# Stacked operand for the gate units of a 64-token tile, and another order of gate units and routing tables

## The chip, the cores and the metric

The kernel runs on one core of a Trainium2 chip. The metric is the device time of one execution in microseconds (us), lower is better. A core has TensorE (PE in the rows: matmuls; its loads of the stationary operand are PEld), VectorE (DVE), ScalarE (ACT), GpSimd (POOL) and SyncE (SP), which here only issues transfers, and 16 DMA engines.

## What is computed

One decoder layer for 512 prompt tokens and 64 sample tokens (8 sequences of 8), D = 1024: attention and a gated short convolution, a projection and a layer norm; then for the normalised tokens `x2` a mixture of experts (64 experts, 6 per token), a shared expert and per-layer embeddings, and a second norm. What matters here is the second half, cut:

```
x2 = h.reshape(n * s, D_MODEL)
eidx, gw = route(x2, lw['w_router'], lw['router_bias'])
ffn = (swiglu(x2, lw['w_s_gate'], lw['w_s_up'], lw['w_s_down'])
       + routed_experts(x2, eidx, gw, lw['w_e_gate'], lw['w_e_up'], lw['w_e_down']))
ple = jax.nn.sigmoid(h @ lw['w_ple_gate']) * (p @ lw['w_ple_proj'])
h = layer_norm(DN_ALPHA * h + ffn.reshape(n, s, D_MODEL) + ple, lw['ln2_g'], lw['ln2_b'])
```

The change touches the product `h @ w_ple_gate` and its sigmoid.

## The kernel before

Every engine has its own program, written out by hand in one order; semaphores join them. The 576 tokens are five tiles, four of 128 and one of 64 (`NT` = 5, the last tile has `NS` = 64). Float32 products are made from split operands: each operand is a high part and a low part (`_hi`, `_lo`), and a product is the sum of three terms, high by high, high by low, low by high.

**Gate units.** The product with `w_ple_gate` is cut into 4 blocks of 256 columns (`GW`) and 5 token tiles: 20 units, numbered u = 5 * block + tile. A unit (`gate_unit`, L1399 to L1412) is 8 chunks of the contraction times 3 terms, 24 matmuls, with the tokens as the stationary operand (128 columns, or 64 for the last tile) and 256 columns of weights moving. Its bank of PSUM is one of two (`gate_bank`), so a unit waits until the sigmoid of the unit two before has read it (`u_sig`). Then Scalar takes the sigmoid into `sig_g` (`gate_sigmoid`, L979 to L986), GpSimd multiplies with the projected embeddings (`ple_product`, `u_mul`), and Vector adds the result to the residual (`ppo_add`). The weights of a block are loaded by SyncE (`load_gate`), Scalar makes the high part (`gate_hi`), Vector the low part (`gate_lo`, `pw_lo`). Two slots hold them, so the load of block 3 waits for unit 9, the last of block 1.

**Block 3** (units 15 to 19) is done in two halves: `last_block(True)` makes the two terms with high tokens for all five tiles, three of them in banks of `att`, and ends with `tb_used`; then the gathered tokens of the first expert pass are turned (`turn(0)`); then `last_block(False)` adds the term with low tokens.

**Routing tables.** Vector builds ten tables, each for three of the 30 (tile, choice) pairs (loop at L2013, rows L2021 to L2028), in two buffers; a table waits until TensorE has multiplied the one two before (`tb_used`). TensorE sums them (`table_products`, L1394) between gate units: `N_AHEAD` = 3 units stand before the first table, and one unit follows each of tables 1, 3, 5 and 7 (`UNIT_AFTER`). Before table 4 Vector also makes the second product of the shared expert (`shared_act(1)`). Behind the tables Vector does `gate_lo(2)`, turns the sums into index tables and raises `routed`.

**Transfers.** SyncE issues in one fixed order; a wait holds back everything behind it:

```
sp.wait_ge(routed, 1)
load_parts(1, 1, range(3))
sp.wait_ge(u_ready, 2 * NT)
load_gate(3)
sp.wait_ge(ppo_added, 1)
load_parts(1, 1, range(3, 5))
sp.wait_ge(hs_hd, 1)
load_parts(1, 1, range(5, 6))
sp.wait_ge(tb_used, NTK // TPAIR + 1)
load_parts(2, 2, range(2))
sp.wait_ge(u_ready, N_BLK * NT)
load_parts(2, 2, range(2, 4))
```

Experts are taken in 32 pairs; the weights of a pair are 6 transfers of 1 MB (gate, up, down, for two experts), in a ring of three slots. Each transfer of a pair also waits until the same part of the pair before has landed. From pair 3 on, a load waits until the pair that held its slot has been used.

**A form that is already there.** In the projection with `w_o`, the 64-token tile is stacked: `smp` holds its 64 high and 64 low columns side by side, a matmul multiplies both at once (`packed` in `tile_products`), and Vector adds the lower 64 rows of the result to the upper.

Of the kernel before, what the change touches and what calls it, by code (L numbers as in the profile page):

```python
# [12 lines left out]
ALU = mybir.AluOpType  # L13
# [42 lines left out]
N_AHEAD = 3  # L56
UNIT_AFTER = (1, 3, 5, 7)
# [64 lines left out]
def decoder_step(nc, x_prompt, x_sample, p_prompt, p_sample, win_k, win_v, conv_state, w_in, sinks,  # L122
# [4 lines left out]
    with ctx:  # L127
# [5 lines left out]
        def sem(name):  # L133
            return ctx.enter_context(nc.semaphore(name))
# [131 lines left out]
        pt_lo = at("pt_lo", [P, 2, T], F32R, o_x + 36352)  # L266
        ppo = [at(f"ppo{i}", [P, NT, 512], F32, o) for i, o in enumerate((o_w1 + 28672, o_w2 + 36864))]
# [135 lines left out]
        pw_in = [sem(f"pw_in{i}") for i in range(2)]  # L403
        pw_hi, pw_lo = sem("pw_hi"), sem("pw_lo")
# [88 lines left out]
        def _(sp):  # L493
# [144 lines left out]
            sp.wait_ge(u_ready, N_BLK * NT)  # L638
# [134 lines left out]
        def _(act):  # L773
# [188 lines left out]
            gate_hi(0)  # L962
            act.wait_ge(lt_mm, 1)
# [16 lines left out]
            def gate_sigmoid(u):  # L980

                w = ntok(u % NT)
                act.wait_ge(u_ready, u + 1)
                if u >= NSIG:
                    act.wait_ge(u_mul, u - NSIG + 1)
                nc.scalar.activation(sig_g[0:w, u % NSIG, :], gate_bank(u)[0:w, :], ACT.Sigmoid).then_inc(u_sig, 1)  # L986
# [59 lines left out]
        def _(pe):  # L1046
# [351 lines left out]

            def gate_unit(u):  # L1399

                j, t = u // NT, u % NT
                w = ntok(t)
                if t == 0:
                    pe.wait_ge(pw_lo, j + 1)
                whi, wlo = (m[GATE_SLOT[j]][:, :].rearrange("p (c n) -> p c n", c=KC) for m in (pg_hi, pg_lo))
                if u >= 2:
                    pe.wait_ge(u_sig, u - 1)
                for c in range(KC):
                    for n, (x, v) in enumerate(((xt_hi, whi), (xt_hi, wlo), (xt_lo, whi))):
                        last = nc.tensor.matmul(gate_bank(u)[0:w, :], x[:, c, t * P:t * P + w], v[:, c, :],  # L1410
                                                start=(c == 0 and n == 0), stop=(c == KC - 1 and n == 2))
                last.then_inc(u_ready, 1)  # L1412
# [11 lines left out]
            def last_block(high):  # L1424

                whi, wlo = (m[GATE_SLOT[3]][:, :].rearrange("p (c n) -> p c n", c=KC) for m in (pg_hi, pg_lo))
                terms = ((xt_hi, whi), (xt_hi, wlo)) if high else ((xt_lo, whi),)
                for t in range(NT):
                    u, w = 3 * NT + t, ntok(t)
                    if high and t == 3:  # L1430
                        pe.wait_ge(u_sig, 3 * NT)
                    for c in range(KC):
                        for n, (x, v) in enumerate(terms):
                            last = nc.tensor.matmul(gate_bank(u)[0:w, :], x[:, c, t * P:t * P + w], v[:, c, :],
                                                    start=(high and c == 0 and n == 0), stop=(not high and c == KC - 1))
                    if not high:
                        last.then_inc(u_ready, 1)
                if high:
                    last.then_inc(tb_used, 1)
# [138 lines left out]
        def _(dve):  # L1578
# [434 lines left out]

            for m in range(NTK // TPAIR):
# [3 lines left out]
                if m >= 2:  # L2018
# [10 lines left out]
                                        ALU.mult).then_inc(tb_ready, 1)  # L2029
            gate_lo(2)  # L2030
# [23 lines left out]
            dve.drain().then_inc(routed, 1)  # L2054

# [19 lines left out]
            for u in range(2 * NT, 3 * NT):  # L2075
                ppo_add(u)
            xt_half(0)
            for u in range(3 * NT, N_BLK * NT):
                last = ppo_add(u)
# [142 lines left out]
```

## Time and profile before

| | us |
|---|---|
| median of 3 runs | 1253.28 |
| lowest, highest | 1251.75, 1253.85 |
| the profiled execution | 1250.78 |
| its span, first to last instruction | 1248.9 |
| TensorE busy in it | 1214.2 (97%) |
| Vector busy in it | 505.8 (40%) |
| Scalar busy in it | 318.7 (26%) |
| GpSimd busy in it | 140.4 (11%) |
| moved by DMA | 307.31 MB, mean 246 GB/s |

TensorE is busy over the whole span, since its pipelined matmuls overlap in the records: the busy share doesn't say that it is the bound. Rows give a start in us from the span's start, a duration, the engine, the line and the operation. The start-to-start distance of matmuls is what a stream costs.

### The profile page before, as it was taken

To read this page: it belongs to the slowest core of one execution; us is meant where nothing else is said; L and a number is where in the kernel's file an instruction comes from. 1 tells how busy PE (TensorE), PEld (TensorE's weight loads), DVE (VectorE), ACT (ScalarE), POOL (GpSimd) and SP (SyncE) were. 2 spreads that over 40 slices of the span, in tenths; PEclk is the share of its full clock that TensorE was granted. 3 is DMA by queue.
4 is the path that set the end of the run, shared out by engine and by line. 5 is a ranking of instruction groups with operands and counts; after the bars stand their busy time and mean duration, and the time that the engine had idled before them with its cause. 6 is when DMAs were issued, how large, how long until landed. Compare 5 with 4: busy or idle time off the path is not lost.

```text
span 1248.9 us, 23615 instructions
## 1 busy us (share of the span) xinstructions
PE 1214.2 (97%) x8816; PEld 958.2 (77%) x8817; DVE 505.8 (40%) x1147; ACT 318.7 (26%) x614; POOL 140.4 (11%) x211
## 2 busy tenths in 40 slices
PE   8999999999999999999999999989999999999887
PEld 8999979999999999998999565556555555556543
DVE  4666783432444323567973112211222222121137
ACT  4364653322211222316012111111111111111121
POOL 0200000000000000003024212111121121221200
PEclk9999999999999999999999999999999999999999
DMA  8222223223222232606347999999999999999996
GB/s 266 79 62 68 68 52 68 68 67 102 68 86 84 68 120 67 213 21 211 146 172 297 420 418 420 421 420 419 420 420 419 422 419 418 420 422 420 421 374 290
DMA packets 98656, 307.31 MB, mean 246 GB/s; under 512 B 11244, under 2 KB 62404, under 8 KB 72840
## 3 DMA queue, kind: packets, MB, share of 16 engines
q1 hardware_dynamic: 85332, 275.20, 56.9%
q0 software_dynamic: 12304, 28.60, 5.9%
q10 hardware_dynamic: 948, 2.50, 0.6%
q8 instruction: 52, 0.85, 0.3%
q14 instruction: 20, 0.16, 0.0%
HBM read 294.45 MB, written 26.94 MB: 257 GB/s over the span
## 4 chain that ended last, share of the span: by engine, by line
PE 49%; DMA 42%; DVE 6%; issue 1%; DVEq 1%; ACT 0%; SPq 0%; POOL 0%; ACTq 0%; POOLq 0%
DMA w_exp<-in_w_e_down_dram 40%; PE proj L1060 32%; PE proj L1270 4%; PE proj L1410 3%; PE att L1192 1%; PE att L1154 1%; PE att L1279 1%; PE proj L1094 1%; DMA fold<-expert_rows 1%; PE att L1205 1%; DVE res L2155 1%; PE att L1270 1%; PE proj L1394 1%; DMA expert_rows<-ysb,sidx_col 1%; DMA x_tok<-in_x_prompt_dram 1%
## 5 line engine op out<-in xcount | busy, mean ns | idle before, releaser
L1481 PE MATMUL att<-w_exp,xt 128*64 128x256 f32 x2560 | 286.3, 380 | 8.7 <-DMA w_exp<-in_w_e_up_dram 6.6
L1481 PEld LDWEIGHTS att<-w_exp,xt 128*64 128x64 f32 x2560 | 189.8, 137 | 114.9 <-issue 36.0
L1060 PE MATMUL proj<-h_hi,w_hi 128*128 128x288 f32 x768 | 167.8, 300 | 0.3 <-DVE w_lo L475 0.3
L1060 PE MATMUL proj<-h_hi,w_lo 128*128 128x288 f32 x768 | 164.0, 295 | 0.0
L1060 PE MATMUL proj<-h_lo,w_hi 128*128 128x288 f32 x768 | 163.9, 295 | 0.0
L1501 PE MATMUL proj<-w_exp,ht_e 128*64 128x512 f32 x640 | 146.2, 598 | 3.8 <-DMA w_exp<-in_w_e_down_dram 3.8
L1060 PEld LDWEIGHTS proj<-h_hi,w_hi 128*128 128x128 f32 x768 | 122.3, 189 | 6.1 <-issue 4.6
L1060 PEld LDWEIGHTS proj<-h_lo,w_hi 128*128 128x128 f32 x768 | 123.6, 188 | 0.0
L1060 PEld LDWEIGHTS proj<-h_hi,w_lo 128*128 128x128 f32 x768 | 123.4, 188 | 0.0
L475 DVE TENSOR_TENSOR w_lo<-w_raw,w_hi 128x2048 fp32r<-128x2048 f32 x33 | 75.6, 2291 | 93.1 <-ACT w_hi L465 88.5
L1501 PEld LDWEIGHTS proj<-w_exp,ht_e 128*64 128x64 f32 x640 | 43.6, 136 | 76.4 <-issue 72.1
L465 ACT ACTIVATE w_hi<-w_raw 128x2048 fp32r<-128x2048 f32 x33 | 63.1, 1911 | 84.5 <-PE proj L1060 73.9
L2102 DVE TENSOR_SCALAR ysb<-proj,tabw 128x512 f32 x40 | 30.0, 751 | 131.7 <-PE proj L1501 131.7
L2097 DVE TENSOR_TENSOR h_e<-sg,att 128x128 f32<-128x128 f32 x80 | 19.5, 285 | 116.8 <-PE att L1481 116.8
L2092 DVE TENSOR_TENSOR sg<-sg,att 128x256 f32<-128x256 f32 x40 | 16.9, 421 | 119.9 <-ACT sg L1012 119.9
L1020 ACT ACTIVATE ysb<-proj,tabw 128x512 f32 x40 | 27.5, 688 | 133.3 <-PE proj L1501 133.3
L1015 ACT ACTIVATE ht_e<-att 128x128 f32<-128x128 f32 x80 | 19.0, 278 | 166.6 <-PE att L1487 166.6
L1420 PEld LDWEIGHTS proj<-ident,xg 128*128 128x128 f32 x328 | 43.6, 196 | 16.5 <-issue 13.8
L1060 PE MATMUL proj<-mix_hi,w_lo 128*128 128x288 f32 x256 | 54.8, 296 | 0.0
L1060 PE MATMUL proj<-mix_hi,w_hi 128*128 128x288 f32 x256 | 54.8, 296 | 0.0
L1060 PE MATMUL proj<-mix_lo,w_hi 128*128 128x288 f32 x256 | 54.8, 296 | 0.0
L1420 PE MATMUL proj<-ident,xg 128*128 128x128 f32 x328 | 53.9, 287 | 0.9 <-DMA xg<-x_rows,gidx_col 0.8
(388 smaller groups left out, 1769.1 us busy)
## 6 DMA issues: line engine op xcount, KB each, us to landing
w_exp<-in_w_e_gate_dram SPq DMA_DIRECT2D x64, 1024.0 KB
w_exp<-in_w_e_up_dram SPq DMA_DIRECT2D x64, 1024.0 KB
w_exp<-in_w_e_down_dram SPq DMA_DIRECT2D x64, 1024.0 KB
w_raw<-in_w_in_dram SPq DMA_DIRECT2D x21, 1024.0 KB
part<-expert_rows SPq DMA_DIRECT2D x8, 1536.0 KB, 20.4
w_raw<-in_w_in_dram SPq DMA_DIRECT2D x8, 512.0 KB
w_raw<-in_w_attn_out_dram SPq DMA_DIRECT2D x8, 512.0 KB
w_raw<-in_w_conv_out_dram SPq DMA_DIRECT2D x4, 1024.0 KB
```

Source lines behind the costliest of these rows:

```text
L465: nc.scalar.activation(w_hi[:, g.par, :], w_raw[:, g.par, :], ACT.Copy).then_inc(hi_done, 1)
L475: nc.vector.tensor_tensor(w_lo[:, g.par, :], w_raw[:, g.par, :], w_hi[:, g.par, :].bitcast(F32), ALU.subtract).then_inc(w_ready, 1)
L1015: nc.scalar.activation(ht_e[:, c, :], att[:, 1 - c, 0:P], ACT.Copy).then_inc(ht_ready, 1)
L1020: nc.scalar.activation(ysb[:, bass.ds(side_of, 1), 0:512].rearrange("p o n -> p (o n)"), proj[:, 2, :], ACT.Copy, scale=tabw[:, bass.ds(k, ...
L1060: last = nc.tensor.matmul(proj[:, 2 * i + a, 0:HALF], lhs, x[:, c, a * HALF:(a + 1) * HALF], start=(c == 0 and n == 0), stop=(c == KC - 1 ...
L1270: last = nc.tensor.matmul(out, x, v, start=(c == 0 and n == 0), stop=(c == KC - 1 and n == last_term))
L1410: last = nc.tensor.matmul(gate_bank(u)[0:w, :], x[:, c, t * P:t * P + w], v[:, c, :], start=(c == 0 and n == 0), stop=(c == KC - 1 and n = ...
L1420: last = nc.tensor.transpose(proj[:, half, c * P:(c + 1) * P], xg[:, :, half * 4 + c], ident[:, :])
L1481: last = nc.tensor.matmul(att[e * SLOT:(e + 1) * SLOT, m, 0:FF], xt[:, c, e * SLOT:(e + 1) * SLOT], weights[e][:, c, :], start=(c == 0), s ...
L1501: last = nc.tensor.matmul(proj[e * SLOT:(e + 1) * SLOT, 2 + half, :], ht_e[:, c, e * SLOT:(e + 1) * SLOT], down[e][:, c, half * 512:(half ...
L2097: nc.vector.tensor_tensor(h_e[:, c:FF:2], sg[:, c:FF:2], att[:, 2, c:FF:2], ALU.mult).then_inc(h_ready, 1)
L2102: nc.vector.tensor_scalar(ysb[:, bass.ds(side_of, 1), 512:D].rearrange("p o n -> p (o n)"), proj[:, 3, :], tabw[:, bass.ds(k, 1)], None, A ...
```

## The change

The 64-token tile's units (4, 9, 14 and 19) get a stacked operand. Scalar copies the tile's high and low columns side by side into `xt_both`; a unit (`packed_unit`) is then 16 matmuls of 128 columns, each with both parts: high weights, then low weights. This makes four terms, the low by low one among them. The two halves of the result, rows 0 to 63 and 64 to 127, are added on Vector (`packed_add`: a copy out of PSUM, a drain, an addition) into `sig_g`, and the sigmoid of these units reads `sig_g` instead of PSUM. Vector's program has the four sums at fixed places: after table 3, after `routed`, before the addition of unit 13, and after the turned tokens have been copied. Unit 19 is complete in the high half of block 3, where it comes first.

The order of units and tables is another: four units before the first table, and one unit after each of tables 0, 2, 4 and 6. SyncE's wait for `u_ready` = 20 becomes 19.

```
-N_AHEAD = 3
-UNIT_AFTER = (1, 3, 5, 7)
+N_AHEAD = 4
+UNIT_AFTER = (0, 2, 4, 6)
...
+        xt_both = at("xt_both", [P, KC, 2, NS], F32R, o_x + 36864)
...
+        packed_sum, PACKED_0 = s_sub, 1
...
-            sp.wait_ge(u_ready, N_BLK * NT)
+            sp.wait_ge(u_ready, N_BLK * NT - 1)
...
             gate_hi(0)
+            act.drain()
+            nc.scalar.activation(xt_both[:, :, 0, :], xt_hi[:, :, SEQ:T].bitcast(F32), ACT.Copy)
+            act.wait_ge(x2_lo, 2 * NT)
+            nc.scalar.activation(xt_both[:, :, 1, :], xt_lo[:, :, SEQ:T].bitcast(F32), ACT.Copy)
+            act.drain()
...
+                if u % NT == NT - 1:
+                    act.wait_ge(packed_sum, PACKED_0 + u // NT + 1)
+                    nc.scalar.activation(sig_g[0:w, u % NSIG, :], sig_g[0:w, u % NSIG, :], ACT.Sigmoid).then_inc(u_sig, 1)
+                    return
...
+            def packed_unit(u, whi, wlo):
+
+                for c in range(KC):
+                    both = xt_both[:, c, :, :].rearrange("p a n -> p (a n)")
+                    for n, v in enumerate((whi, wlo)):
+                        last = nc.tensor.matmul(gate_bank(u), both, v[:, c, :],
+                                                start=(c == 0 and n == 0), stop=(c == KC - 1 and n == 1))
+                return last
...
-                for t in range(NT):
-                    u, w = 3 * NT + t, ntok(t)
+                if high:
+                    pe.wait_ge(u_sig, N_BLK * NT - 6)
+                    packed_unit(N_BLK * NT - 1, whi, wlo)
+                for t in range(NT - 1):
+                    u = 3 * NT + t
...
+            def packed_add(u):
+
+                if u == N_BLK * NT - 1:
+                    dve.wait_ge(tb_used, NTK // TPAIR + 1)
+                else:
+                    dve.wait_ge(u_ready, u + 1)
+                dve.wait_ge(u_mul, u - NSIG + 1)
+                o, total = gate_bank(u), sig_g[0:NS, u % NSIG, :]
+                nc.vector.tensor_copy(total, o[NS:P, :])
+                dve.drain()
+                nc.vector.tensor_tensor(total, total, o[0:NS, :], ALU.add).then_inc(packed_sum, 1)
...
+                if m == 3:
+                    packed_add(NT - 1)
...
             dve.drain().then_inc(routed, 1)
+            packed_add(2 * NT - 1)
...
             for u in range(2 * NT, 3 * NT):
+                if u == 3 * NT - 2:
+                    packed_add(3 * NT - 1)
                 ppo_add(u)
             xt_half(0)
+            packed_add(N_BLK * NT - 1)
             for u in range(3 * NT, N_BLK * NT):
```

Vector's program around tables 3 and 4 (`tab_a` and `tab_b` are a table's two operands, `hs_f` the shared expert's product). Before:

```order
L2021 TENSOR_TENSOR tab_b<-cc_152,col_j 128x3x90 [waits tb_used]
L2023 TENSOR_TENSOR tab_a<-cc_152,slot_j 128x384
L2026 TENSOR_TENSOR tab_b<-tab_b,cc_152 128x3x90
L2028 TENSOR_TENSOR tab_b<-tab_b,wj 128x3x90
L1950 TENSOR_TENSOR hs_f<-att,hs_f 128x576 [waits ss_ready]
L1952 TENSOR_TENSOR hs_f<-att,hs_f 128x576
L2021 TENSOR_TENSOR tab_b<-cc_152,col_j 128x3x90 [waits tb_used]
```

Now:

```order
L2058 TENSOR_TENSOR tab_b<-cc_153,col_j 128x3x90 [waits tb_used]
L2060 TENSOR_TENSOR tab_a<-cc_153,slot_j 128x384
L2063 TENSOR_TENSOR tab_b<-tab_b,cc_153 128x3x90
L2065 TENSOR_TENSOR tab_b<-tab_b,wj 128x3x90
L2047 COPY sig_g<-proj 64x256 [waits u_mul,u_ready]
L2049 TENSOR_TENSOR sig_g<-sig_g,proj 64x256
L1975 TENSOR_TENSOR hs_f<-att,hs_f 128x576 [waits ss_ready]
L1977 TENSOR_TENSOR hs_f<-att,hs_f 128x576
L2058 TENSOR_TENSOR tab_b<-cc_153,col_j 128x3x90 [waits tb_used]
```

The sum of unit 4 stands between table 3 and the shared product, with table 4 behind both.

TensorE's program at the last tables (a table is three matmuls, `x2` is a row of two; the row behind them is the first matmul of the next unit). Before, tables 8 and 9 behind unit 6:

```order
L1394 MATMUL proj<-tab_b,tab_a 128x180 [waits tb_ready]
L1394 MATMUL proj<-tab_b,tab_a 128x180 x2
L1394 MATMUL proj<-tab_b,tab_a 128x180 [waits tb_ready]
L1394 MATMUL proj<-tab_b,tab_a 128x180 x2
L1410 MATMUL proj<-pg_hi_150,xt_hi 128x256 [waits u_sig]
```

Now, tables 7, 8 and 9 behind unit 7:

```order
L1405 MATMUL proj<-tab_b,tab_a 128x180 [waits tb_ready]
L1405 MATMUL proj<-tab_b,tab_a 128x180 x2
L1405 MATMUL proj<-tab_b,tab_a 128x180 [waits tb_ready]
L1405 MATMUL proj<-tab_b,tab_a 128x180 x2
L1405 MATMUL proj<-tab_b,tab_a 128x180 [waits tb_ready]
L1405 MATMUL proj<-tab_b,tab_a 128x180 x2
L1432 MATMUL proj<-pg_hi_151,xt_hi 128x256 [waits u_sig]
```

Table 7 has moved behind one more unit, and three tables stand in a row at the end.

## Rows read from the trace of the kernel before

**Rows 1.** Chain of waits (start us, us, what): two TensorE stretches, the first transfer.

```profile
630.27 2.73 PE proj L1410 x24
...
644.25 22.73 PE proj L1410 x192
...
684.67 10.41 DMA w_exp<-in_w_e_down_dram
```

**Rows 2.** Windows: length, busy PE, PEld, DVE, ACT, POOL; clock, DMA share, GB/s.

```profile
652.00:660.00 8.00, 8.00 (x69) 8.00 (x68) 0.54 (x2) 1.15 (x3) 2.34 (x4) 1.00 1.03 400
671.00:677.00 6.00, 6.00 (x54) 6.00 (x53) 0.00 (x0) 0.00 (x0) 0.35 (x1) 1.00 0.45 184
...
820.00:840.00 20.00, 17.60 (x113) 10.14 (x115) 4.22 (x9) 3.22 (x8) 3.86 (x7) 1.00 1.02 421
```

**Rows 3.** Timeline of SyncE's queue: start us, us to issue, line, transfer, count.

```profile
648.05 0.81 SPq L596 DMA_DIRECT2D w_exp<-in_w_e_gate_dram  x2
...
652.76 0.38 SPq L588 DMA_DIRECT2D pg_raw<-in_w_ple_gate_dram  x1
...
676.51 0.81 SPq L596 DMA_DIRECT2D w_exp<-in_w_e_gate_dram  x2
682.14 0.80 SPq L596 DMA_DIRECT2D w_exp<-in_w_e_up_dram  x2
```

**Rows 4.** Timeline of TensorE, 64-token tile stacked in the projection with `w_o`.

```profile
522.65 0.28 PE L1270 MATMUL att<-w_lo,smp 128*128 128x256 f32 x1
...
524.33 0.28 PE L1270 MATMUL att<-w_lo,smp 128*128 128x256 f32 x1
```

**Rows 5.** Timeline of Vector, from table 3 to the low half of gate block 2.

```profile
626.09 0.43 DVE L2021 TENSOR_TENSOR tab_b<-cc,col_j 128x270 f32<-128x270 f32 x1
...
627.94 0.75 DVE L1950 TENSOR_TENSOR hs_f<-att,hs_f 128x576 f32<-128x576 f32 x1
...
629.45 0.51 DVE L2021 TENSOR_TENSOR tab_b<-cc,col_j 128x270 f32<-128x270 f32 x1
...
633.96 0.56 DVE L2021 TENSOR_TENSOR tab_b<-cc,col_j 128x270 f32<-128x270 f32 x1 [0.65 <-PE proj L1394]
...
642.50 2.29 DVE L1893 TENSOR_TENSOR pg_lo<-pg_raw,pg_hi 128x2048 fp32r<-128x2048 f32 x1
```

**Rows 6.** Timeline of TensorE: tables (L1394), gate units (L1410), last block (L1434).

```profile
622.53 1.18 PE L1394 MATMUL proj<-tab_b,tab_a 128*128 128x180 f32 x6 [1.66 <-DVE tab_b L2028]
...
632.84 1.99 PE L1394 MATMUL proj<-tab_b,tab_a 128*128 128x180 f32 x12
634.55 0.41 PE L1410 MATMUL proj<-pg_hi,xt_hi 128*128 128x256 f32 x1
...
637.55 2.00 PE L1394 MATMUL proj<-tab_b,tab_a 128*128 128x180 f32 x12
...
666.81 0.28 PE L1434 MATMUL att<-pg_hi,xt_hi 128*128 128x256 f32 x1
```

**Rows 7.** Timeline of Vector: an addition of 64 tokens by 256 columns.

```profile
653.99 0.42 DVE L2063 SCALAR_TENSOR_TENSOR res<-res,ppo 64x256 f32<-64x256 f32 x1 [1.87 <-POOL ppo L706]
```

**Rows 8.** Timelines of Scalar and Vector: the two splits of gate block 3.

```profile
660.94 1.92 ACT L960 ACTIVATE pg_hi<-pg_raw 128x2048 fp32r<-128x2048 f32 x1 [2.03 <-DMA pg_raw<-in_w_ple_gate_dram]
...
662.88 2.29 DVE L1893 TENSOR_TENSOR pg_lo<-pg_raw,pg_hi 128x2048 fp32r<-128x2048 f32 x1 [8.48 <-ACT pg_hi L960]
```

**Rows 9.** Scalar: the copy into `smp` (by tile), and the logits' copy (timeline).

```profile
L912 ACT ACTIVATE smp<-merged_hi x1: 636/636/636, 508.9 to 508.9; 128x512 fp32r<-128x512 f32 x1
...
584.78 0.65 ACT L964 ACTIVATE lt<-proj 128x576 f32<-128x576 f32 x1 [1.86 <-PE proj L1344]
```

**Rows 10.** Timeline of GpSimd: the first gather of tokens.

```profile
660.80 1.13 POOL L721 DMA_INDIRECT xg<-x_rows,gidx_col  x1 [0.95 <-POOL gidx_col L718]
```

**Rows 11.** Waits of TensorE: us in total, times, longest us.

```profile
PE att L1481 <- DMA w_exp<-in_w_e_up_dram: 6.6, 5, 2.1
...
PE proj L1394 <- DVE tab_b L2028: 2.3, 2, 1.7
```

More of the change, by code:

```diff
@@ L985, in gate_sigmoid @@
                     act.wait_ge(u_mul, u - NSIG + 1)
-                nc.scalar.activation(sig_g[0:w, u % NSIG, :], gate_bank(u)[0:w, :], ACT.Sigmoid).then_inc(u_sig, 1)
+                nc.scalar.activation(sig_g[0:w, u % NSIG, :], gate_bank(u), ACT.Sigmoid).then_inc(u_sig, 1)
             for u in range(N_BLK * NT):
@@ L1397, in table_products @@
                 last.then_inc(tb_used, 1)
+            def packed_unit(u, whi, wlo):
[5 more added lines that the diff above has]
+                return last
             def gate_unit(u):
                 j, t = u // NT, u % NT
-                w = ntok(t)
                 if t == 0:
@@ L1407, in gate_unit @@
                     pe.wait_ge(u_sig, u - 1)
[L1408 to L1411, printed above, removed]
+                if t == NT - 1:
+                    last = packed_unit(u, whi, wlo)
+                else:
+                    for c in range(KC):
+                        for n, (x, v) in enumerate(((xt_hi, whi), (xt_hi, wlo), (xt_lo, whi))):
+                            last = nc.tensor.matmul(gate_bank(u), x[:, c, t * P:(t + 1) * P], v[:, c, :],
+                                                    start=(c == 0 and n == 0), stop=(c == KC - 1 and n == 2))
                 last.then_inc(u_ready, 1)
@@ L1433, in last_block @@
                         for n, (x, v) in enumerate(terms):
-                            last = nc.tensor.matmul(gate_bank(u)[0:w, :], x[:, c, t * P:t * P + w], v[:, c, :],
+                            last = nc.tensor.matmul(gate_bank(u), x[:, c, t * P:(t + 1) * P], v[:, c, :],
                                                     start=(high and c == 0 and n == 0), stop=(not high and c == KC - 1))
@@ L2012, in _ @@
             dve.drain()
+            def packed_add(u):
+                if u == N_BLK * NT - 1:
+                    dve.wait_ge(tb_used, NTK // TPAIR + 1)
+                else:
+                    dve.wait_ge(u_ready, u + 1)
[4 more added lines that the diff above has]
+                nc.vector.tensor_tensor(total, total, o[0:NS, :], ALU.add).then_inc(packed_sum, 1)
             for m in range(NTK // TPAIR):
```

## Prediction

> **What bounds the kernel now.** I read the chain of waits first. From 684.67 us it consists of expert-weight transfers, one behind the other; before that it is TensorE's: the tables and gate units, 22.73 us for the last eight units before the fourth gate block [rows 1]. The windows give the reason: in the expert stage the DMA engines move 421 GB/s at a share of 1.02 while TensorE has room (17.60 of 20 us busy), but from 671 to 677 us they move only 184 GB/s [rows 2]. So the stream of experts cannot be shortened by TensorE, but it can start earlier or later. It starts with the issue of pair 2's gate weights at 676.51 us, which waits for `tb_used` = 11, the end of the high half of the fourth gate block (`last_block(True)`, first matmul at 666.81) [rows 3, 6]. Call that end X. Before the change X is 676.5; what X moves, the end moves, one for one. Work ahead of it counts only if it reaches X.
>
> **What the change removes.** A unit of the 64-token tile had 24 matmuls, 2.73 us [rows 1]; stacked, it has 16 of 128 columns. The kernel already has that form in its third projection: the second stacked matmul starts at 522.65, the last at 524.33, so 14 steps are 1.68 us, 0.12 each [rows 4]. Sixteen make 1.92 us: 0.81 us less. Three of the four such units lie before `last_block(True)`: 2.4 us. The fourth had 16 matmuls in the high half (about 16/24 x 2.73 = 1.82) and now has 16 of 0.12 (1.92): +0.1 us for X; its 8 in the low half (0.9 us) are gone behind X. If nothing else waited, X would come 2.3 us sooner.
>
> **The tables' order.** A table takes Vector 1.85 us (626.09 to 627.94), the shared product 1.51 (to 629.45), and one that waits for its buffer starts 1.12 us after TensorE began the table that frees it: TensorE's first matmul of tables 4 and 5 is at 632.84, Vector goes on at 633.96 [rows 5, 6]. From such a start to readiness I take 2.05 us, the pace of 1.85 and a little for the restart and the last instruction's end. Two tables hold TensorE 1.71 us (632.84 to 634.55), one 0.86, and a full unit behind tables 3.00 (to 637.55) [rows 6]; a stacked one is then 2.04. From these I walk the new order (units start at 612.1 as before: 622.53, less the wait of 1.66 and three units of 2.88).
> - Four units: table 0 starts at 623.6 (it is ready at 622.5, so the wait of 1.66 us [rows 6] is gone). Stacked unit to 626.5, tables 1 and 2, unit 5 to 631.2. Vector's table 3 now waits for table 1, which stands behind a unit: it starts at 627.6 and is ready at 629.5, instead of 628.0.
> - Then Vector does the stacked unit's sum. The nearest row is 0.42 us for 64x256 [rows 7]; two of them and a drain make 0.85 us (bounds 0.5 to 1.2; a negative cost is excluded, since they are added instructions). With the shared product, table 4 starts at 631.75 and is ready at 633.8. TensorE, through with table 3 at 632.05, waits 1.75 us.
> - Unit 6 to 637.7, tables 5 and 6, unit 7 to 642.4. Table 9's buffer is freed by table 7, which now stands behind unit 7: Vector starts it at 643.5, ready at 645.6. TensorE is through with table 8 at 644.1 and waits 1.5 us.
>
> So TensorE starts unit 8 at 646.5 instead of about 646.9: waits of 2.3 us [rows 11] have become 3.25, and that eats the first stacked unit's gain. Worse, Vector leaves the tables at 645.5, where its low half of gate block 3 (`pg_lo`) started at 642.50 before [rows 5]: 3.0 us later.
>
> **Where those 3 us go.** Behind the tables Vector needs 5.55 us to `routed` (642.50 to the issue at 648.05) [rows 3, 5]; now `routed` comes at 651.05. SyncE waits for it in order, issues three expert transfers, and only then loads the fourth gate block. Before, that load was issued at 652.76 (unit 9's end) and landed at 660.94, where Scalar's split starts; Vector's ends at 665.17, and TensorE came at 666.81, 1.6 us later [rows 3, 8]. Now unit 9 ends at 651.7, the issue is at 652.4. Three expert transfers and this one are 4.19 MB; at the 400 GB/s of that stretch [rows 2] they take 10.5 us, which is what lies between the start of the flow near 649.6 and the landing, with about 0.9 left. So the landing hangs on `routed`, not on its own issue: 12.9 us behind it, at 663.9. With 4.2 us for the two splits, `pw_lo` = 4 comes at 668.1. The last-but-one stacked unit also waits, since Scalar's split stands before the sigmoid that frees its bank: to 665.9, so it ends at 667.8. Free of both, TensorE would come at 646.5 + 5 x 2.88 + 2 x 1.92 + 0.1 = 664.8. It starts `last_block(True)` at 668.1, 1.3 us later than before; with the +0.1, X = 677.9.
>
> By the issue-to-landing time alone (8.2 us), the load would land at 660.6, and X would be PE's, 2.0 us earlier than before. The Trainium skill, "DMA: Bandwidth & Descriptors", section "Queues, rings and completion order", says that each DMA engine consumes the descriptors of one ring in ring order. By that rule the fourth block stands behind the three expert transfers of the same issuer, and the flow above agrees; it speaks against this change.
>
> **Edits at nothing.** Scalar's two copies into the stacked operand stand before the copy of the logits. A copy of that size took 0.636 us, and Scalar idles 1.86 us before `lt` at 584.78 [rows 9]; 1.27 us and two drains fit, and TensorE has two chunks of shared work besides. The sums behind `routed` and in the two runs of additions are 0.85 us each on Vector; the additions they delay free only pair 1's last transfers, in which the DMA has 6 us at 184 GB/s before X. The last one comes after the turned tokens and now waits for the multiply of unit 17: `res_done` comes some 2 us later behind X, but pair 2's down weights, which need it, queue behind 4 MB. The up weights were issued 5.63 us behind X (682.14) [rows 3]; the low half is 8 matmuls shorter, so 0.9 us sooner, which closes a thin place in the flow: I take -0.2 us (0 to -0.6).
>
> **Sum.** +1.3 + 0.1 - 0.2 = +1.2 us. The profiled execution took 1250.78 us with a span of 1248.9; it would take 1252.0, span 1250.1. The median of the runs shown, 1253.28, lies 2.5 us above it; with it the forecast is **1254.5 us**.
>
> **Rivals.**
> - Landing is early (the load isn't held by the three before it, or Vector's tables are less late than I walk). X is set by TensorE: -2.0 + 0.1 - 0.2 = -2.1 us, 1251.2. For it speaks that no row shows four loads issued so close; against it the measured flow. Chance 0.14.
> - The gather of the first tokens runs in the same stretch. GpSimd issued it at 660.80, after the landing [rows 10]; now unit 11 is done earlier against the transfers, the issue is near 659.7, and its 0.5 MB at 400 GB/s can add up to 1.3 us before the landing; Vector's sum at its upper bound of 1.2 us adds 0.35. At most +1.6, taken as +1.5: 1256.0. Chance 0.16.
> - The clock falls, and the kernel is slower. TensorE would idle 2.9 us before the stacked unit 14 (662.9 to 665.9), longer than any wait in the list of waits (the longest 2.1 us [rows 11]); at those the granted clock stayed at 1.00, the level of 2.4 GHz [rows 2]. If it went to 1.2 GHz, the spacing of 0.12 us would double; over the 80 matmuls up to X that is 9.6 us, over half of them 4.8: 1259.3. It decides where that idle time is longer than the clock bears. Chance 0.06. The Trainium skill, "TensorE: Matmul & The Clock Gate", section "HAM oscillation", warns that idle gaps throttle TensorE; no wait in this trace shows it.
> - The change doesn't do what it says (the stacked unit costs as much as before): +0.8 on each, of which the first delays table 9 and `routed` by up to 0.8: 1255.3, inside the range. Chance 0.02.
>
> **How the numbers follow.** Forecast 0.62, early landing 0.14, gather 0.16, clock 0.06, no saving 0.02. A measurement of this kernel can tell about 0.2%, 2.5 us: 1250.8 and 1255.8 are the edges. A tenth of the forecast's chance, over half of the gather's and all of the clock's fall above: 0.06 + 0.09 + 0.06 = 0.21. Below falls a third of the early landing's and a little else: 0.07. The range reaches from the early landing to the gather with its upper bound, 1251.0 to 1257.0; outside are the clock and the tails.
>
> **What would show it.** Right: stacked matmuls 0.12 us apart; TensorE waits of 1 to 2 us before tables 4 and 9, none before 0; `routed` 3 us later; the fourth gate block landing near 664; TensorE idle before unit 14 and before `last_block(True)`; X at 677 to 679. Wrong: a landing before 662, table 9 ready before 644, or an expert stream whose end doesn't move with X.

## The result: slower by 0.46%, and the profile after

| | before | after |
|---|---|---|
| median of 7 runs each, us | 1251.75 | 1257.43 |
| lowest, highest | 1250.86, 1253.85 | 1256.64, 1259.38 |
| ratio, 95% interval | | 1.0046 [1.0034, 1.0057] |
| the profiled execution, us | 1250.78 | 1258.67 |
| its span | 1248.9 | 1256.8 |
| X, from the span's start | 676.51 | 683.81 |
| from X to the end of the span | 572.4 | 573.0 |
| mean granted clock | 0.998 | 0.993 |

The forecast was +1.2 us and no difference that can be measured; it became +5.7 in the medians and 7.9 in the profiled executions. The end followed X, as forecast: X came 7.3 us later, not 1.4. Of two kernels further below, e9 and e11, one execution each took 5612 and 4730 us; their ratios leave it out.

SyncE's queue after the change (start us, us to issue, line, transfer, count), which answers to [rows 3]:

```profile
652.74 0.80 SPq L598 DMA_DIRECT2D w_exp<-in_w_e_gate_dram  x2
653.58 0.43 SPq L598 DMA_DIRECT2D w_exp<-in_w_e_up_dram  x1
654.06 0.66 SPq L590 DMA_DIRECT2D pg_raw<-in_w_ple_gate_dram  x1
...
683.81 1.26 SPq L598 DMA_DIRECT2D w_exp<-in_w_e_gate_dram  x2
```

The first row is `routed`, the third the load of the fourth gate block, the last is X. TensorE's timeline, which answers to [rows 6] (tables are now L1405, full units L1432, stacked ones L1415, the last block L1459; in brackets the wait ahead and what ended it):

```profile
623.71 1.08 PE L1405 MATMUL proj<-tab_b,tab_a 128*128 128x180 f32 x6
624.50 0.41 PE L1415 MATMUL proj<-pg_hi,xt_both 128*128 128x256 f32 x1
...
634.47 2.17 PE L1405 MATMUL proj<-tab_b,tab_a 128*128 128x180 f32 x6 [2.15 <-DVE tab_b L2065]
636.20 0.65 PE L1432 MATMUL proj<-pg_hi,xt_hi 128*128 128x256 f32 x1
...
639.93 2.00 PE L1405 MATMUL proj<-tab_b,tab_a 128*128 128x180 f32 x12
...
647.87 1.18 PE L1405 MATMUL proj<-tab_b,tab_a 128*128 128x180 f32 x6 [1.24 <-DVE tab_b L2065]
648.77 0.41 PE L1432 MATMUL proj<-pg_hi,xt_hi 128*128 128x256 f32 x1
...
669.36 0.58 PE L1415 MATMUL proj<-pg_hi,xt_both 128*128 128x256 f32 x1 [4.00 <-ACT sig_g L997]
669.75 0.42 PE L1415 MATMUL proj<-pg_lo,xt_both 128*128 128x256 f32 x1
669.96 0.41 PE L1415 MATMUL proj<-pg_hi,xt_both 128*128 128x256 f32 x1
670.17 0.41 PE L1415 MATMUL proj<-pg_lo,xt_both 128*128 128x256 f32 x1
```

Two things are to be seen. The waits are where the prediction put them, before tables 4 and 9 and before unit 14; only the one before the last block didn't come. And behind two of them matmuls are slow: table 4 holds TensorE from 634.47 to 636.20, 1.73 us, where a table holds it 0.86; unit 6 takes 3.73 us (to 639.93) instead of 3.00; in unit 14 matmuls are 0.21 us apart instead of 0.12. The windows, which answer to [rows 2] (length, busy PE, PEld, DVE, ACT, POOL; clock, DMA share, GB/s), name the cause:

```profile
634.50:637.50 3.00, 3.00 (x12) 3.00 (x12) 2.44 (x6) 1.76 (x1) 0.00 (x0) 0.50 0.00 0
...
666.00:668.00 2.00, 0.00 (x0) 0.00 (x0) 0.00 (x0) 0.87 (x1) 0.00 (x0) 1.00 1.00 409
670.00:674.00 4.00, 4.00 (x20) 4.00 (x20) 3.91 (x6) 0.00 (x0) 2.82 (x2) 0.50 0.18 74
676.00:678.00 2.00, 2.00 (x19) 2.00 (x19) 0.07 (x1) 0.00 (x0) 1.10 (x3) 1.00 0.53 106
820.00:840.00 20.00, 17.42 (x110) 9.93 (x108) 3.04 (x6) 2.15 (x5) 2.45 (x4) 0.91 1.02 421
```

The granted clock was 0.50, the level of 1.2 GHz, from 634.5 to 637.5 us behind the wait of 2.15 us, and again behind the wait of 4.00. Before the change it was above 0.98 in every 20-us window of the trace up to 1240 us; only in the last one, in which the program ends, it was 0.85. The busy share doesn't show this: a slow TensorE counts as busy.

The splits of the fourth gate block, on Scalar and on Vector (two timelines), which answer to [rows 8]:

```profile
667.13 1.91 ACT L962 ACTIVATE pg_hi<-pg_raw 128x2048 fp32r<-128x2048 f32 x1 [7.10 <-DMA pg_raw<-in_w_ple_gate_dram]
```

```profile
669.07 2.29 DVE L1918 TENSOR_TENSOR pg_lo<-pg_raw,pg_hi 128x2048 fp32r<-128x2048 f32 x1 [9.68 <-ACT pg_hi L962]
```

And the chain of waits (start us, us, what), which answers to [rows 1]; before the change TensorE's units filled this stretch without a break:

```profile
654.06 13.05 DMA pg_raw<-in_w_ple_gate_dram
667.24 1.71 issue
668.95 0.38 ACT sig_g L997
669.36 6.74 PE proj L1415 x32
676.10 5.75 PE att L1459 x48
```

The load of the block is now itself a piece of the chain, 13.05 us long.

### The profile page after: what moved, and what is told of

It reads as the page before. It is cut to its first block, busy times and chain, and to the rows that moved or that the text cites. A ratio compares the mean times of both kernels' runs of the same rounds, so it can differ in the third digit from the quotient of the medians.

```text
span 1256.8 us, 23568 instructions
## 1 busy us (share of the span) xinstructions
PE 1217.6 (97%) x8784; PEld 961.3 (76%) x8785; DVE 507.0 (40%) x1155; ACT 319.9 (25%) x616; POOL 141.0 (11%) x211
## 4 chain that ended last, share of the span: by engine, by line
PE 51%; DMA 42%; DVE 4%; issue 1%; DVEq 1%; SPq 0%; ACT 0%; ACTq 0%; POOLq 0%
DMA w_exp<-in_w_e_down_dram 38%; PE proj L1071 32%; PE proj L1281 4%; PE proj L1432 1%; PE att L1203 1%; PE att L1165 1%; PE att L1290 1%; PE proj L1105 1%; DMA pg_raw<-in_w_ple_gate_dram 1%; DMA fold<-expert_rows 1%; PE proj L1376 1%; PE att L1376 1%; PE att L1216 1%; PE proj L1415 1%; PE att L1459 1%
```

## The experiments

My theory after the result had three causes, all of which delay X: the fourth block's load stands behind three expert transfers that wait for `routed`; `routed` is late because Vector's sum and the single tables hold up table 4; and the clock falls in the waits that these two make. The rivals: the new order or the stacked units by themselves; a clock that doesn't matter; the first gather of tokens.

All runs in one table. Traces lie up to 2.1 us apart before the first gate unit, so routed, the start of the fourth block's split, and X are counted from the start of that unit (F; 612.08 before, 612.19 after). Where SyncE loads the block before it waits for `routed`, its queue doesn't show when `routed` came, and the cell is empty. "Clock" tells in which of the 20-us windows from 620 and from 660 the granted clock fell, and to what.

| kernel | median us | ratio [95%] | routed | split | X | clock | X to end |
|---|---|---|---|---|---|---|---|
| before | 1251.75 | 1 | 35.97 | 48.86 | 64.43 | 1.00 | 572.4 |
| after | 1257.43 | 1.0046 [1.0034, 1.0057] | 40.55 | 54.94 | 71.62 | 0.91, 0.83 | 573.0 |
| e1, bridged | 1256.37 | 1.0019 [1.0005, 1.0033] | 38.97 | 53.29 | 67.65 | 1.00 | 572.4 |
| e2, block first | 1253.06 | 0.9996 [0.9982, 1.0010] | | 47.71 | 64.70 | 0.91, 1.00 | 572.3 |
| e3, old order | 1251.53 | 0.9988 [0.9976, 1.0001] | 37.47 | 50.24 | 64.61 | 0.91, 1.00 | 572.5 |
| e4, order alone | 1257.44 | 1.0030 [1.0017, 1.0043] | 38.89 | 53.41 | 69.74 | 1.00, 0.91 | 572.3 |
| e5, early sum | 1258.14 | 1.0046 [1.0030, 1.0061] | 38.36 | 52.58 | 68.11 | 1.00, 0.91 | 573.9 |
| e6, e5 + block first | 1250.81 | 0.9981 [0.9971, 0.9991] | | 45.52 | 62.52 | 1.00 | 574.3 |
| e7, e3 + block first | 1251.97 | 0.9995 [0.9982, 1.0007] | | 47.36 | 64.35 | 0.91, 1.00 | 572.1 |
| e8, before + block first | 1253.22 | 1.0000 [0.9986, 1.0014] | | 47.89 | 65.60 | 0.91, 1.00 | 572.3 |
| e9, tables in pairs | 1256.54 | 1.0023 [1.0012, 1.0033] | 37.49 | 51.68 | 68.32 | 1.00, 0.83 | 572.8 |
| e10, e9 + block first | 1250.39 | 0.9975 [0.9964, 0.9986] | | 44.57 | 61.57 | 1.00 | 572.5 |
| e11, before bridged | 1253.99 | 1.0007 [0.9996, 1.0017] | 36.92 | 51.14 | 65.85 | 1.00 | 572.5 |
| e12, gather late | 1256.66 | 1.0033 [1.0020, 1.0046] | 40.54 | 54.98 | 70.33 | 0.92, 0.91 | 573.6 |
| e13, before, gather early | 1253.51 | 1.0010 [0.9995, 1.0025] | 35.59 | 50.97 | 65.70 | 1.00 | 572.2 |

Each ratio is against runs of the kernel before on the same chip (medians 1253.4 to 1253.7 for the experiments).

**Does the clock matter?** The waits stay, idle matmuls fill them; these compute nothing that is used.

```
             for m in range(NTK // TPAIR):
+                if m == 4:
+                    keep_busy(7)
                 table_products(m)
...
             for u in range(N_AHEAD + len(UNIT_AFTER), 3 * NT):
+                if u == 3 * NT - 1:
+                    keep_busy(16)
                 gate_unit(u)
```

> The changed kernel, with idle matmuls (identity by identity into a free bank, result unused) where TensorE waited longest: 7 before table 4, 16 before unit 14. Waits, sums and transfers stay. Clock theory: the granted clock stays at 1.00 in both places. Table 4 and unit 6 then cost 3.9 us instead of 5.5, so table 9, the index tables and the fourth gate block's load come 1.6 us sooner; unit 14 and unit 19 cost 3.9 instead of 6.6 us, another 2.6. X (the issue of pair 2's gate weights) goes from 683.8 to about 679.6 us and the time to about 1.5 us above the kernel before (ratio 1.001). Rival, the clock is only a symptom and the transfer decides: X stays within 1 us of 683.8.

Two windows of its trace:

```profile
620.00:640.00 20.00, 19.40 (x152) 19.21 (x151) 15.90 (x33) 3.87 (x6) 3.68 (x5) 1.00 0.61 239
660.00:680.00 20.00, 19.57 (x164) 19.20 (x163) 5.97 (x8) 3.93 (x5) 7.45 (x7) 1.00 0.67 252
```

The clock stayed at 1.00, and X came at 679.60 instead of 683.81, just what the theory of the clock gave; against F it is 4.0 us of the 7.2 by which the change had moved X. The dependences are the same, only the idle time is gone. The median moved less, by a ratio of 1.0046 to 1.0019: in its other executions the mean clock was 0.994 to 0.999, which fits falls elsewhere, but no trace of them is kept.

**Does the landing matter?** SyncE loads the fourth block before it waits for `routed`.

```
-            sp.wait_ge(routed, 1)
-            load_parts(1, 1, range(3))
             sp.wait_ge(u_ready, 2 * NT)
             load_gate(3)
+            sp.wait_ge(routed, 1)
+            load_parts(1, 1, range(3))
```

> The changed kernel, with one exchange in SyncE's program: the load of gate block 3 (waits for unit 9) stands before the wait for routed and the three expert transfers. Theory of the queue: the load lands 5 to 6 us after its issue, near 659.5 instead of 667.1, TensorE doesn't wait before unit 14 or the last block, the second fall of the clock goes too, and X comes at 676.6 to 677 instead of 683.8: the time is that of the kernel before within 1 us (ratio 1.000). The first fall of the clock, before table 4, stays. Rival, the landing is late for another cause (the gather, bandwidth): the landing stays after 664 and X after 681.

From its trace, SyncE's queue and Scalar's split:

```profile
655.43 0.38 SPq L590 DMA_DIRECT2D pg_raw<-in_w_ple_gate_dram  x1
655.92 0.99 SPq L598 DMA_DIRECT2D w_exp<-in_w_e_gate_dram  x2
...
678.47 1.26 SPq L598 DMA_DIRECT2D w_exp<-in_w_e_gate_dram  x2
```

```profile
661.48 1.90 ACT L962 ACTIVATE pg_hi<-pg_raw 128x2048 fp32r<-128x2048 f32 x1
```

The block landed some 5.4 us after its issue instead of 13.1, the split started 7.2 us earlier against F, and the wait before unit 14 was gone, and with it the second fall of the clock. X came 6.9 us earlier against F; the whole loss but 0.3 us was recovered, with the first fall still in it.

**The order or the stacked units?** First the stacked units in the old order, then the new order without stacked units:

```
-N_AHEAD = 4
-UNIT_AFTER = (0, 2, 4, 6)
+N_AHEAD = 3
+UNIT_AFTER = (1, 3, 5, 7)
...
-                if m == 3:
+                if m == 5:
                     packed_add(NT - 1)
```

> The changed kernel with the old order: three units before the first table, one after tables 1, 3, 5 and 7; unit 4's sum stands after table 5, since unit 4 now follows table 3. Stacked units stay. Theory that the order and the place of the sum are the harm and stacking the gain: no wait over 1.8 us before a table, clock at 1.00, table 9 ready about 0.8 us sooner than in the kernel before, landing near 660, TensorE free or nearly free of it, X at 674 to 675 against 676.5: 1.5 to 2.5 us faster than the kernel before (ratio 0.9985). Rival, the stacked units and their sums are themselves the harm: X at or after 678, slower by 1.5 us or more.

```
-N_AHEAD = 3
-UNIT_AFTER = (1, 3, 5, 7)
+N_AHEAD = 4
+UNIT_AFTER = (0, 2, 4, 6)
```

> The kernel before with the new order alone (four units ahead, one after tables 0, 2, 4 and 6), no stacking and no sums. Theory: table 1 stands behind unit 4 of 2.86 us, table 3 is ready near 630.4 and table 4 near 633.8 with the shared product between, TensorE, through with table 3 at 632.9, waits 0.9 us: no fall of the clock. Table 9 waits for table 7 as in the changed kernel: ready near 646 to 646.5, routed at 651.7, the fourth gate block lands at 664.6 to 666, TensorE waits less for it since its two 64-token units take longer; X at 678.5 to 680, 2 to 3.5 us slower than the kernel before (ratio 1.002). Rival, the sum before table 4 is the whole harm: X within 0.7 us of 676.5.

The old order with stacked units is not slower than before; its median moved as expected (a ratio of 0.9988, expected 0.9985), but X did not: 0.2 us later against F, where I had expected 1.5 to 2.5 earlier. The order alone costs most of the loss: X + 5.3 us against F, where I had expected 2 to 3.5, and a ratio of 1.0030, whose interval overlaps that of the changed kernel. The split started 14.5 us behind `routed` instead of 12.9, and TensorE's wait before unit 14 was 3.33 us long, in which the clock fell:

```profile
669.46 0.33 PE L1410 MATMUL proj<-pg_hi,xt_hi 128*64 128x256 f32 x1 [3.33 <-ACT sig_g L986]
```

In e3's trace the clock fell where I had not expected it, at table 1, behind waits of 1.65 and 0.67 us. The kernel before had the same waits (1.66 and 0.66) without a fall, and its table 1 took 1.18 us, not 2.17:

```profile
622.97 1.18 PE L1405 MATMUL proj<-tab_b,tab_a 128*128 128x180 f32 x6 [1.65 <-DVE tab_b L2065]
624.82 2.17 PE L1405 MATMUL proj<-tab_b,tab_a 128*128 128x180 f32 x6 [0.67 <-DVE tab_b L2065]
```

**Vector's sum.** Its place is moved to where Vector waits for table 1 anyway (e5), and then the block is loaded first as well (e6).

```
-                if m == 3:
+                if m == 2:
                     packed_add(NT - 1)
```

> The changed kernel with one move: Vector's sum of the first stacked unit (unit 4) stands after table 2, where Vector waits for TensorE's table 1 in any case, instead of after table 3. Theory (a wait of 2.15 us before table 4 and the clock falling there, then Vector's tables late): the wait before table 4 becomes about 1.3 us, the granted clock stays higher in 620 to 640, table 4 and unit 6 are 1.6 us shorter, X (issue of pair 2's gate weights, 683.8 in the changed kernel) comes at 680.5 to 682; the landing of the fourth gate block and the fall before unit 14 stay; time about 1255 us. Rival (only the landing behind the three expert transfers counts, the sum's place does not): X at 683 to 684, 1257.4 us.

> The same, and SyncE loads the fourth gate block before it waits for the routing, so ahead of the three expert transfers. Theory: both delays are gone, the splits end near 663, TensorE waits neither before unit 14 nor before the fourth block; what is left is the number of TensorE's instructions, 32 fewer than before: X at 674 to 676, time 1249.5 to 1251.5 us, about 0.2 per cent below the kernel before. Rival (the expert stream is what counts, so that its three transfers issued later cost at the end what X gains): X earlier as said, but the time within 0.5 us of the kernel before's, with a wait for expert weights in pair 0 or 1.

In e5's trace the wait before table 4 is 1.52 us, the clock stays up there, and X is 680.26, just ahead of the 680.5 to 682 expected:

```profile
633.80 1.18 PE L1405 MATMUL proj<-tab_b,tab_a 128*128 128x180 f32 x6 [1.52 <-DVE tab_b L2065]
```

Of its 3.5 us against F, 2.2 are an earlier `routed`; most of the rest is a second fall of the clock that was shorter here (0.91, not 0.83), though the wait ahead of it was 3.84 us long. The time did not follow: 1258.14, a ratio of 1.0046 as in the changed kernel. In the trace 1.5 us are lost behind X, where the clock fell from 1180 to 1220 us, and the mean clock of its five executions is low, 0.991 to 0.994; why isn't known. So the trace shows what the sum's place does to `routed`, but no time shows a gain by it alone. In e6 the whole is recovered and more: ratio 0.9981, X 1.9 us earlier against F than in the kernel before; its interval overlaps that of e2.

**Controls of the early load.** The same edit in the old order with stacked units, and in the kernel before.

> The stacked units in the old order of units and tables (three units ahead, one after tables 1, 3, 5 and 7), with the fourth gate block loaded before the wait for the routing. Theory (in the old order the fourth block was only 1.6 us ahead of TensorE, with the stacked units TensorE reaches it at about the same time, so the earlier load saves little): X 674 to 676 against 677.1 without the earlier load, time 1250 to 1251.5 us. Rival (landing did not matter in the old order): X at 677, time as without it.

> The kernel before, with only the load of the fourth gate block ahead of the wait for the routing. Theory (in the kernel before the landing was 1.6 us ahead of the need, so it bound nothing): X stays at 676 to 677, time within 0.1 per cent of the kernel before. The three expert transfers are issued some 4 us later, after unit 9, and wait for nothing else. Rival (whoever loads the fourth block first wins, stacked or not): X and the time 1 us or more earlier; or slower by 1 us or more, if the later expert transfers hold up pair 0 or 1.

In the old order the early load brings nothing: X moves 0.3 us with stacked units (the rival held; I had expected 1 to 3), the time of the kernel before not at all (its X is 1.2 us later here, in a trace in which the clock fell at table 1). In these two pairs of kernels the block's load binds only where the new order has made `routed` late.

**Single tables or four units ahead?** Four units stay ahead, but the others follow tables 1, 3, 5 and 7 again (e9); then with the block first (e10).

```
 N_AHEAD = 4
-UNIT_AFTER = (0, 2, 4, 6)
+UNIT_AFTER = (1, 3, 5, 7)
```

> The changed kernel with four units ahead of the tables, but one unit after each of tables 1, 3, 5 and 7, as before. It tells apart the two parts of the new order: four units ahead, and tables single and in pairs. Theory (a single table between units leaves each pair of buffers behind a unit, and that makes the waits of 2.15 and 1.24 us; the late fourth gate block makes the rest): no wait before table 0, waits before the later tables at most 1.1 us, routing raised at 649 (652.7 in the changed kernel, 648.0 before), unit 8 at 645 (648.8). TensorE gets to unit 14 at 661 and waits there 3 to 4 us for the split of the fourth gate block, since that still lands 13 to 14 us behind the routing, at 662 to 663.5; the clock falls in the wait: X 679 to 681, time 1255 us. Rival (four units ahead are themselves too late for Vector): routing at 651 or later, X at 683.

> The same with the fourth gate block loaded ahead of the wait for the routing. Theory: the block is there at 659, its splits end at 663, TensorE comes at 663 to 663.5 without a long wait: X 672.5 to 674, about 1 us earlier than with the single tables, an early sum and the same early load (674.6), and 3 us earlier than in the kernel before; time 1249 to 1250 us, the fastest of all. Rival (from here on the experts' first transfers bound, issued after unit 9): X as early, but the time at 1250.8 or above.

X came out as the theory had it in both (680.32 and 673.63). The time of e9, 1256.54 us, is 1.5 us above what I had said, and that of e10 0.4. TensorE's waits in e10 (us in total, times, longest) and its SyncE queue:

```profile
PE proj L1405 <- DVE tab_b L2065: 1.5, 3, 1.0
```

```profile
650.59 0.38 SPq L590 DMA_DIRECT2D pg_raw<-in_w_ple_gate_dram  x1
651.07 0.99 SPq L598 DMA_DIRECT2D w_exp<-in_w_e_gate_dram  x2
...
673.63 0.80 SPq L598 DMA_DIRECT2D w_exp<-in_w_e_gate_dram  x2
```

`routed` comes 3.1 us earlier than after the change (e9, 37.49 against 40.55), of which 1.6 us are the clock that now stays up at table 4 and unit 6. No wait for a table is longer than 1.03 us, and the clock is above 0.98 in every 20-us window of e10 up to 1240 us. X is at 673.63, 2.9 us before that of the kernel before. e10 has the lowest median here: ratio 0.9975 [0.9964, 0.9986], 1250.39 us (I had said 1249 to 1250); from e6, 0.9981, the intervals don't tell it apart.

**Does the clock also fall in the kernel before?** Idle matmuls, which compute nothing that is used, fill its waits before tables 0 and 1.

```
             for m in range(NTK // TPAIR):
+                if m == 0:
+                    for _ in range(12):
+                        nc.tensor.matmul(proj[:, 0, 0:P], ident[:, :], ident[:, :], start=True, stop=True)
+                if m == 1:
+                    for _ in range(5):
...
                 table_products(m)
```

> The kernel before, with 12 idle matmuls ahead of table 0 and 5 ahead of table 1, which compute nothing that is used; they fill its waits of 1.66 and 0.65 us. The question is whether the clock also falls at table 0 in some executions of the kernel before, which would be a part of its spread. Theory (the wait of 1.66 us lowers it in some executions, by 1.6 us of time each, as in the trace with the old order and stacked units): granted clock 1.00 in 620 to 640, X at 676.5, median 0.5 to 1 us below the kernel before. Rival (no effect): same median within 0.3 us.

No gain: 1.0007 [0.9996, 1.0017], so the theory isn't supported. The run showed something else: the block's split started 14.2 us behind `routed`, not 12.9, and X was 1.4 us later against F than in the trace of the kernel before, with the same instructions but the idle ones. `routed` was 1.0 us later too (36.92 against 35.97), so not all of the 1.4 us is the landing's.

```profile
663.31 1.91 ACT L960 ACTIVATE pg_hi<-pg_raw 128x2048 fp32r<-128x2048 f32 x1 [3.36 <-DMA pg_raw<-in_w_ple_gate_dram]
```

**The gather.** It is moved behind the multiply of unit 13 in the changed kernel, and ahead, behind that of unit 9, in the kernel before.

```
-            gather(0, 0, 1)
             for u in range(2 * NT + 2, 3 * NT):
+                if u == 3 * NT - 1:
+                    gather(0, 0, 1)
                 ple_product(u)
```

> The changed kernel with GpSimd's first gather of tokens issued behind the multiply of unit 13, so after the fourth gate block has landed, instead of behind that of unit 11 (661.92). In the changed kernel and five others the block landed 14.2 to 14.5 us after the routing and 5.0 to 5.2 MB were moved by then; in the kernel before and one other 12.8 to 12.9 us and 4.4 to 4.6 MB, and in these two the gather was issued within 0.8 us of the landing. Theory (the gather costs the landing 1.4 us, though few of its own bytes move by then): landing 12.9 us after the routing, X 1.4 us earlier than in the changed kernel, about 682.3, time about 1256 us. Rival (the gather has no part in it, the transfers behind the block run ahead of its last packets): landing 14.2 to 14.5 us after the routing, X 683 to 684, time 1257.4 us.

> The mirror: the kernel before with the first gather issued behind the multiply of unit 9, near 655, some 6 us ahead of the landing instead of 0.1 us. Theory (gather): landing 14.2 to 14.5 us after the routing instead of 12.9, the splits end near 666.7, X at 677.5 to 678, time 1 us above the kernel before. Rival: landing 12.9 us after the routing or without relation to the gather, time as before.

With the gather at 675.97, long after the landing, the split still started 14.4 us behind `routed`. So the gather isn't what makes the changed kernel's landing late; X was 1.3 us earlier, nearly the 1.4 of the theory, but for another reason: the clock fell for a shorter time (0.91 in the second window, not 0.83). In the mirror the split came 15.4 us behind `routed`: all 0.38 MB of the gather had moved by then, 1.0 us at the 360 GB/s of that stretch, on top of 14.4. So a gather inside the stretch seems to cost its bytes (one trace, and its ratio, 1.0010 [0.9995, 1.0025], shows no loss of time); in the changed kernel at most 0.08 MB of it had moved before the landing.

## Where the prediction was right and where it failed

**Right.** The bound: from X to the end it is 572.1 to 573.0 us in all but three traces; those three (573.6 to 574.3) have the clock down somewhere between 1160 and 1220 us. The ring: the block's load is held by the three expert transfers, and its landing hangs on `routed`; e2 shows it by moving one line. The walk of the tables: table 0 at 623.71 without a wait (623.6 forecast), waits of 2.15 and 1.24 us before tables 4 and 9 (1.75 and 1.5). The small terms, too, among them Vector's sum of 0.85 us:

```profile
629.61 0.43 DVE L2047 COPY sig_g<-proj 64x256 f32<-64x256 f32 x1
630.11 0.41 DVE L2049 TENSOR_TENSOR sig_g<-sig_g,proj 64x256 f32<-64x256 f32 x1
630.45 0.74 DVE L1975 TENSOR_TENSOR hs_f<-att,hs_f 128x576 f32<-128x576 f32 x1
...
631.94 0.97 DVE L2058 TENSOR_TENSOR tab_b<-cc,col_j 128x270 f32<-128x270 f32 x1
```

It takes 0.84 us (629.61 to 630.45). A stacked unit behind a table takes 2.02 us (624.50 to 626.52; 2.04 forecast), the copies of the tokens are hidden (the logits' copy at 584.89, before 584.78).

**Wrong: the sum of +1.2.** The account of X, forecast 677.9, measured 683.8:

- `routed` at 652.7 instead of 651.05, +1.65. Table 4 and unit 6 at half clock are 1.6 of it; table 4 was ready 0.6 later than walked, since Vector began it 0.2 later and its first operation took 0.97 us instead of 0.51 (last row above, against [rows 5]); behind the tables Vector needed 5.0 us to `routed` instead of 5.55, -0.55.
- The landing 14.4 us behind `routed` instead of 12.9, +1.5. This is the term that was mis-sized: I took it from one trace, and the step "4.19 MB at 400 GB/s, 0.9 left" took for granted that nothing behind the block moves ahead of its last packet. In the before trace and in e3's 4.4 to 4.6 MB had moved on SyncE's queue by then, in all the others where the block stands behind the experts 5.05 to 5.2 MB. Two rows of the DMA view show it (packets, MB, share of 16 engines), from `routed` to the landing, of before (648.0 to 660.9) and of after (652.7 to 667.1):

```profile
q1 hardware_dynamic: 1515, 4.55, 95.1%
```

```profile
q1 hardware_dynamic: 1579, 5.07, 93.4%
```

   Vector's split ends at 671.4 instead of 668.1: these two and 0.1.
- Unit 14 and the stacked half of unit 19 took 6.58 us (669.36 to 675.94) instead of 3.84, at half clock: +2.7. In the forecast the end of Vector's split bound the last block, 0.3 us behind unit 14; here unit 14 was the later one, and TensorE didn't wait again.

These make 5.9 us, the whole difference between 677.9 and 683.8. The term behind X, -0.2 us, did not come either: the up weights came 4.73 us behind X instead of 5.63, as forecast, but from X to the end it took 573.0 us instead of 572.4, in a trace whose clock also fell near 824 us.

**The step that failed** is the rival of the clock. The mechanism stood there, with the right place and about its price (unit 14 idle for 2.9 us, +4.8 if half of the matmuls up to X are slow; it was 4.0 us, and +2.7; the matmuls from unit 14 to X are 96, not the 80 counted), and I gave it 0.06, with the reason that no wait of the list had lowered the clock. But the longest of those was 2.1 us and stood in the expert stage; a wait of 2.9 us was outside of what the trace had shown, which is a reason for a wide range, not for a small chance. I also applied it at one place only. My own walk had a second wait, 1.75 us before table 4, longer than any that TensorE had met in this stage, and it cost 1.6 us, since it lay ahead of `routed`. Together the two falls are 4.3 of the 5.9 us. The rule of the Trainium skill that I had cited, "TensorE: Matmul & The Clock Gate", section "HAM oscillation", that idle gaps throttle TensorE, was right here behind the waits of 2.15 and 4.00 us, and I had set it aside for want of a row.

**The gather rival**, which I had blamed for a late landing, is not its cause (e12). The early landing didn't come. The time of 1257.4 lies 0.4 above the range, whose upper end rested on the gather's price and left the clock out.

## What to carry to other kernels

Where a reordering makes an engine wait for longer than the trace of before has shown it to wait, price the slow matmuls behind each such wait, not the wait alone, and as a chance, since the same wait lowers the clock in one execution and not in another. A load in a shared, ordered queue is as late as the latest wait ahead of it: move it ahead of a wait that it doesn't need before changing what produces that wait; here this one edit took a loss of 0.46% back, and with the tables in pairs it became a gain of 0.25%. When two buffers join producer and consumer, give the consumer's other work after both (pairs), so that one unit covers two tables; here `routed` came 3.1 us sooner by it, half of that through the clock.

## What the runs showed of the chip

- The granted clock fell to the level of 1.2 GHz behind waits of TensorE of 2.15 us (after, e2, e12) and of 3.3 to 4.1 us (after, e4, e5, e9, e12). A 20-us window at 0.91 has 3.6 us at half clock, one at 0.83 has 6.8; only waits of 3.9 us and more had the latter, and not all of them (e12, 4.05 us, had 0.91). Shorter waits did not decide it: 1.52 us left it at 1.00 in e5 and e6; 1.66 and 0.66 us before tables 0 and 1 left it at 1.00 in the kernel before, 1.65 and 0.67 lowered it in e3; 0.74 and 1.19 us lowered it in e8, 0.74 and 1.20 did not in e13.
- Nor does a longer wait decide it, as other stages of the same fifteen traces show. A wait of 2.3 to 2.7 us for expert weights near 820 us stands in eleven of them; behind it the clock fell in seven (after, e2, e3, e5, e6, e9, e11) and stayed up in four (e1, e7, e10, e12). One of 2.0 to 2.2 us near 1180 us lowered it in three of fifteen (e5, e6, e12), one of 1.65 us near 174 us in four of fifteen (e2, e4, e6, e12). Two rows of the first kind, of e3 (clock 0.79 from 818 to 826 us) and of e7 (1.00), with the same 32 matmuls:

```profile
817.89 5.36 PE L1506 MATMUL att<-w_exp,xt 128*64 128x256 f32 x32 [2.57 <-DMA w_exp<-in_w_e_up_dram]
```

```profile
816.74 3.67 PE L1506 MATMUL att<-w_exp,xt 128*64 128x256 f32 x32 [2.54 <-DMA w_exp<-in_w_e_up_dram]
```

  So that each wait of 2.15 us and more between the tables and X was followed by a fall is what eight waits showed, not a limit. What tells the cases apart stays open.
- The landing of a load behind others in one queue varies by 1.3 us with the same transfers (12.9 us behind `routed` in the kernel before, 14.2 in e11). In the later cases some 0.6 MB more of the same queue had moved, which must belong to transfers issued behind the block. The Trainium skill, "DMA: Bandwidth & Descriptors", section "Why a DMA increments its semaphore by 16 and not by 1", says that the engines of a transfer finish independently; that fits the bytes, but why the engines were further apart in most executions isn't settled.
- Vector's operation on 270 elements took 0.97 us at 631.94 and 0.44 at 627.64, the first one beside a multiply of GpSimd; the two were not separated by an experiment.
- Executions of the same kernel differ by up to 7 us (the kernel before, 1250.0 to 1257.1) with mean clocks of 0.999 down to 0.992; a single trace is one of these, and the 12.9 us above came from one near the low end, at 1250.78 us.
